# Seven quarter-block products in place of eight for fourteen feed-forward up chunks

## What is computed

```python
D_MODEL, SEQ, D_FF, CONV_WIDTH = 1024, 256, 2816, 3

def _conv_ffn(h, w_up, conv_w, conv_b, w_down):
    up = h @ w_up                       # (256, 1024) @ (1024, 5632)
    C = up.shape[-1]
    rhs = conv_w.reshape(CONV_WIDTH, 1, C).astype(up.dtype)
    up = lax.conv_general_dilated(up, rhs, window_strides=(1,), padding=[(CONV_WIDTH - 1, 0)],
                                  dimension_numbers=('NWC', 'WIO', 'NWC'),
                                  feature_group_count=C) + conv_b
    gate, val = up[..., :D_FF], up[..., D_FF:]
    return (jax.nn.silu(gate) * val) @ w_down
```

## Time and profile before

| | |
|---|---|
| Time, median of 3 runs | 1548.72 us (1547.1 to 1551.06) |
| Time of the profiled execution | 1549.08 us |
| Span of the profiled execution, first to last instruction | 1547.3 us |
| Feed-forward stage on TensorE in the trace | 248.9 to 472.5 us (first up chunk from 241.2) |
| Granted TensorE clock | 0.999 of 2.4 GHz |

### The profile page before, as it was taken

The page is one execution under the profiler, slowest core; times in us unless marked ns, Lnnn a source line. Parts: engine busy times, 40 slices in busy tenths (PEclk is TensorE's granted clock), DMA queues, the critical chain, the costliest instruction groups (busy, mean ns, idle before and its releaser), DMA issues.

```text
span 1547.3 us, 18178 instructions
## 1 busy us (share of the span) xinstructions
PE 1506.0 (97%) x7042; PEld 835.2 (54%) x7042; DVE 468.2 (30%) x894; ACT 320.4 (21%) x660; POOL 22.4 (1%) x43
## 2 busy tenths in 40 slices
PE   9999999999999999899999899999989999999998
PEld 8667888888888755443333243433324433433432
DVE  3665125665642243512121121211211212121112
ACT  2443142111112453211011011101101101110112
POOL 0000000000000000000000000000000000000000
PEclk9999999999999999999999999999999999999999
DMA  9635444777652255899999999999999999999996
GB/s 379 282 111 200 152 167 164 270 274 269 270 194 58 105 216 203 349 399 430 427 428 427 429 419 416 429 427 429 429 428 427 407 427 429 418 429 427 427 429 274
DMA packets 46720, 513.52 MB, mean 332 GB/s; under 512 B 5264, under 2 KB 5408, under 8 KB 8384
## 3 DMA queue, kind: packets, MB, share of 16 engines
q1 hardware_dynamic: 41984, 482.53, 76.1%
q0 software_dynamic: 4672, 30.06, 5.1%
HBM read 511.51 MB, written 1.06 MB: 331 GB/s over the span
## 4 chain that ended last, share of the span: by engine, by line
PE 84%; DMA 11%; DVE 2%; ACT 1%; issue 1%; DVEq 0%; SPq 0%; ACTq 0%
PE bank L1369 33%; PE bank L745 13%; PE bank L1005 9%; DMA ring<-in_up_w 5%; DMA ring<-in_gate_w 5%; PE bank L1014 5%; PE bank L1333 3%; PE bank L1401 3%; PE bank L1491 3%; PE bank L1220 2%; PE bank L856 2%; PE bank L1386 2%; DMA ring<-in_down_w 1%; PE bank L1173 1%; PE bank L1162 1%
## 5 line engine op out<-in xcount | busy, mean ns | idle before, releaser
L1369 PE MATMUL bank<-ring,probs_slab 128*64 128x512 f32 x2824 | 634.9, 597 | 20.4 <-DMA ring<-in_gate_w 11.5
L1369 PEld LDWEIGHTS bank<-ring,probs_slab 128*64 128x64 f32 x2824 | 193.2, 137 | 393.6 <-issue 359.7
L1005 PE MATMUL bank<-normed,ring 128*128 128x256 f32 x672 | 146.9, 379 | 0.0
L2586 DVE TENSOR_TENSOR squares<-bank,tab 128x512 f32<-128x512 f32 x31 | 21.4, 692 | 412.0 <-PE bank L1386 412.0
L1005 PEld LDWEIGHTS bank<-normed,ring 128*128 128x128 f32 x672 | 127.5, 190 | 18.1 <-issue 0.8
L745 PE MATMUL bank<-normed,ring 128*128 128x256 f32 x384 | 84.5, 381 | 0.4 <-ACT normed L1656 0.4
L745 PEld LDWEIGHTS bank<-normed,ring 128*128 128x128 f32 x384 | 72.1, 190 | 11.7 <-ACT normed L1656 1.2
L1014 PE MATMUL bank<-big_slab,ring 128*128 128x256 f32 x352 | 77.6, 379 | 0.0
L1014 PEld LDWEIGHTS bank<-big_slab,ring 128*128 128x128 f32 x352 | 66.9, 190 | 9.1
L2594 DVE TENSOR_TENSOR squares<-bank,tab 128x512 f32<-128x512 f32 x31 | 21.4, 692 | 157.0 <-PE bank L1386 157.0
L2357 DVE SCALAR_TENSOR_TENSOR big_slab<-bank,residual,big_slab 128x255 f32<-128x255 f32 x84 | 40.5, 482 | 83.0 <-ACT big_slab L1818 80.8
(11 more groups left out here) (396 smaller groups left out, 1299.2 us busy)
## 6 DMA issues: line engine op xcount, KB each, us to landing
ring<-in_down_w SPq DMA_DIRECT2D x61, 2048.0 KB, 16.8
ring<-in_up_w SPq DMA_DIRECT2D x60, 2048.0 KB, 18.9
ring<-in_gate_w SPq DMA_DIRECT2D x58, 2048.0 KB, 18.3
ring<-in_front_w SPq DMA_DIRECT2D x72, 1024.0 KB, 5.2
held_slab<-in_mod_w POOLq DMA_DIRECT2D x6, 1024.0 KB, 8.7
memory_slab<-in_mod_w POOLq DMA_DIRECT2D x6, 1024.0 KB, 8.0
cross_keys_slab<-in_mod_w POOLq DMA_DIRECT2D x6, 1024.0 KB, 6.3
probs_turned_slab<-in_mod_w POOLq DMA_DIRECT2D x6, 1024.0 KB, 7.2
```

What stands on the lines that cost most here:

```text
L1005: mm = pe.matmul(bank[bank_at][:, half * T:(half + 1) * T], w[:, (half * DC + k) * P:(half * DC + k + 1) * P], H[:, k, :], start=(k == 0), ...
L1369: mm = pe.matmul(to[half * SLOTS:(half + 1) * SLOTS, :], tokens(k), weights[:, half * D + i * HALF:half * D + (i + 1) * HALF], start=(k == ...
```

## The change

Fourteen up chunks (`SEVEN`: 4 to 11 and 16 to 21) are computed by a scheme of Strassen's kind. The chunk is seen as a 2x2 by 2x2 block product: input features in two halves of 512, output in gate and value, tokens in two halves of 128. In place of eight quarter products there are seven, each four 128x128 blocks of weights against 128 tokens, of sums of quarters of the weights (t1, t2, t4, and one written over the chunk itself in the ring) with sums of quarters of the input (s1 to s4, made once). The results are combined by sums.

VectorE makes the input sums at f = 1, the weight sums of chunk f+2 in the turn of chunk f (four additions of 128x512), and the merge of chunk f (three additions of 128x128 and one of 128x256 that reads PSUM). ScalarE copies parts of the product from PSUM in three steps: `read_first` after the first quarter product, `read_shared` after the fourth, `read_own` at the end. A chunk uses two banks instead of one; two pairs of banks alternate. The combined product lies in `ff_u` in SBUF (one quarter written by `read_own`, three by the merge), and `ff_base` and `ff_taps` read it from there. In ScalarE's order `ff_base(f-1)` now stands behind `read_first(f)`; in VectorE's, `ff_taps(f)` stands behind the gate of f-1 and the weight sums, and the modulation steps behind the taps.

The slabs `HOLD`, `SQ` and `VX` hold the sums, so the modulation has three slabs, its steps are spread anew over the chunks (`MODULATED_AT`), and the three `DFT` transfers are issued when the last up chunk is done, behind all modulation slabs on GpSimd's queue.

```diff
+SEVEN = list(range(4, 12)) + list(range(16, FF_CHUNKS))
+WEIGHT_SUMS, MERGES, _n = {}, {}, 4
+for _f in range(1, FF_CHUNKS):
+    if _f in SEVEN:
+        MERGES[_f] = _n
+        _n += 4
+    if _f + 2 in SEVEN:
+        WEIGHT_SUMS[_f + 2] = _n
+        _n += 4
+MODULATED_AT = {1: [0], 2: [1, 2], 3: [3], 5: [4], 7: [5], 9: [6], 10: [7], 12: [8, 9], 13: [10], 14: [11, 12],
+                15: [13, 14], 16: [15], 17: [16], 18: [17, 18], 19: [19], 20: [20, 21], 21: [22, 23]}
...
-        mod_w = [flat(s, 0, DC) for s in (HOLD, M, KX, PT)]
+        mod_w = [flat(s, 0, DC) for s in (M, KX, PT)]
...
+        ff_b = [[wide(HOLD, 0), wide(HOLD, 2), wide(HOLD, 4)], [wide(HOLD, 6), wide(SQ, 0), wide(SQ, 2)]]
+        ff_a = [wide(VX, 2 * i).rearrange("p (k t) -> p k t", k=4) for i in range(4)]
+        ff_u = [wide(SQ, 4), wide(SQ, 6)]
+        ff_read = [wide(BIG, 14), ff_second_read]
...
-                pool.dma_start(mod_w[n % 4], mod_w_in[n]).then_inc(mod_here[n % 4], 16)
+                pool.dma_start(mod_w[n % 3], mod_w_in[n]).then_inc(mod_here[n % 3], 16)
 
             full(pool, "vx11")
             load_mod(0)
+            pool.wait_ge(s_cross_scored, XHEADS)
             load_mod(1)
-            pool.wait_ge(s_cross_scored, XHEADS)
+            full(pool, "co3")
             load_mod(2)
-            full(pool, "co3")
-            load_mod(3)
+            pool.dma_start(router_w, router_w_in).then_inc(s_in["wr"], 16)
+            pool.dma_start(router_b, router_b_in.partition_broadcast(P)).then_inc(s_in["wr"], 16)
+            for n in range(3, MOD_ROUNDS * DC):
+                pool.wait_ge(s_mod, mod_steps(n - 2))
+                load_mod(n)
+            pool.wait_ge(s_ff_up, FF_CHUNKS)
             pool.dma_start(DFT[:, 0:5, :], dft_in[:, 0:5, :]).then_inc(s_in["dft"], 16)
             pool.dma_start(DFT[:, 6:8, :], dft_in[:, 5:7, :]).then_inc(s_in["dft"], 16)
             pool.dma_start(DFT[:, 5, :], fourier_w_in).then_inc(s_in["dft"], 16)
-            pool.dma_start(router_w, router_w_in).then_inc(s_in["wr"], 16)
-            pool.dma_start(router_b, router_b_in.partition_broadcast(P)).then_inc(s_in["wr"], 16)
-            for n in range(4, MOD_ROUNDS * DC):
-                pool.wait_ge(s_mod, mod_steps(n - 3))
-                load_mod(n)
...
+            def ff_bank_free(f):
+                if f - 2 in SEVEN:
+                    pe.wait_ge(s_ff_sums, MERGES[f - 2] + 4)
+                    pe.wait_ge(s_ff_read, 3 * SEVEN.index(f - 2) + 3)
+                else:
+                    pe.wait_ge(s_ff_conv, f - 1)
+            def ff_seven(f, w):
+                i = SEVEN.index(f)
+                own, shared = bank[2 * (f % 2)], bank[2 * (f % 2) + 1]
+                t1, t2, t4 = ff_b[i % 2]
+                s1, s2, s3, s4 = ff_a
+                def product(to, b, a, start=False):
+                    for k in range(4):
+                        mm = pe.matmul(to, b[:, k * P:(k + 1) * P], a[:, k, :], start=(start and k == 0), stop=True,
+                                       skip_group_check=True)
+                    return mm
+                product(own[:, 0:P], weight_part(w, 0, 0), token_half(0, 0), start=True).then_inc(s_ff_seven, 1)
+                pe.wait_ge(s_ff_sums, WEIGHT_SUMS[f] + 4)
+                product(shared[:, 0:P], t2, s2, start=True)
+                product(shared[:, P:2 * P], weight_part(w, 0, 1), s3)
+                product(shared[:, 2 * P:3 * P], t1, s1).then_inc(s_ff_seven, 1)
+                pe.wait_ge(s_ff_read, 3 * i + 1)
+                product(own[:, 0:P], weight_part(w, 1, 0), token_half(1, 0))
+                pe.wait_ge(s_ff_read, 3 * i + 2)
+                product(shared[:, 2 * P:3 * P], weight_part(w, 1, 1), s4)
+                product(shared[:, P:2 * P], t4, token_half(1, 1)).then_inc(s_ff_up, 1)
...
-                pe.wait_ge(s_ff_conv, 10 + i)
+                pe.wait_ge(s_ff_conv, 11 + i)
...
+            def read_first(f):
+                i = SEVEN.index(f)
+                act.wait_ge(s_ff_seven, 2 * i + 1)
+                if i >= 2:
+                    act.wait_ge(s_ff_sums, MERGES[SEVEN[i - 2]] + 4)
+                act.activation(ff_read[i % 2][:, 0:P], bank[2 * (f % 2)][:, 0:P], ACT.Copy).then_inc(s_ff_read, 1)
+            def read_shared(f):
+                i = SEVEN.index(f)
+                act.wait_ge(s_ff_seven, 2 * i + 2)
+                act.activation(ff_read[i % 2][:, P:4 * P], bank[2 * (f % 2) + 1][:, 0:3 * P],
+                               ACT.Copy).then_inc(s_ff_read, 1)
+            def read_own(f):
+                i = SEVEN.index(f)
+                act.wait_ge(s_ff_up, f + 1)
+                if i >= 2:
+                    act.wait_ge(s_ff_conv, SEVEN[i - 2] + 1)
+                act.activation(ff_u[i % 2][:, 0:P], bank[2 * (f % 2)][:, 0:P], ACT.Copy).then_inc(s_ff_read, 1)
+                act.wait_ge(s_ff_read, 3 * i + 3)
             ff_base(0, 0, 0, True)
-            for f in range(1, 4):
-                ff_base(f, f, f, True)
-                ff_silu(f - 1, f - 1)
-            for f in range(4, FF_CHUNKS):
-                ff_base(f, f % 4, f, False)
+            for f in range(1, FF_CHUNKS):
+                if f in SEVEN:
+                    read_first(f)
+                if f - 1 in SEVEN:
+                    ff_base(f - 1, (f - 1) % 4, f - 1, False)
+                if f in SEVEN:
+                    read_shared(f)
+                else:
+                    ff_base(f, f % 4, f, f < 4)
                 ff_silu(f - 1, (f - 1) % 4)
+                if f in SEVEN:
+                    read_own(f)
                 if f == 11:
                     act.wait_ge(s_mod_sum, 1)
                     act.activation(mod_n[0], bank[1][:, :], ACT.Copy).then_inc(s_mod_read, 1)
+            if FF_CHUNKS - 1 in SEVEN:
+                ff_base(FF_CHUNKS - 1, (FF_CHUNKS - 1) % 4, FF_CHUNKS - 1, False)
...
+            def ff_input_sums():
+                s1, s2, s3, s4 = ff_a
+                dve.tensor_tensor(s1, token_half(0, 1), token_half(1, 1), ADD).then_inc(s_ff_sums, 1)
+                dve.tensor_tensor(s3, token_half(0, 0), token_half(0, 1), SUB).then_inc(s_ff_sums, 1)
+                dve.wait_ge(s_ff_sums, 1)
+                dve.tensor_tensor(s2, s1, token_half(0, 0), SUB).then_inc(s_ff_sums, 1)
+                dve.wait_ge(s_ff_sums, 3)
+                dve.tensor_tensor(s4, token_half(1, 0), s2, SUB).then_inc(s_ff_sums, 1)
+            def ff_weight_sums(f):
+                i = SEVEN.index(f)
+                w, slot, here = ff_ring(f)
+                t1, t2, t4 = ff_b[i % 2]
+                dve.wait_ge(chunk_here[slot], here)
+                if i >= 2:
+                    dve.wait_ge(s_ff_up, SEVEN[i - 2] + 1)
+                b00, b10, b01, b11 = [weight_part(w, k_half, half) for half in range(2) for k_half in range(2)]
+                dve.tensor_tensor(t1, b01, b00, SUB).then_inc(s_ff_sums, 1)
+                dve.wait_ge(s_ff_sums, WEIGHT_SUMS[f] + 1)
+                dve.tensor_tensor(b01, b11, b01, SUB).then_inc(s_ff_sums, 1)
+                dve.tensor_tensor(t2, b11, t1, SUB).then_inc(s_ff_sums, 1)
+                dve.wait_ge(s_ff_sums, WEIGHT_SUMS[f] + 3)
+                dve.tensor_tensor(t4, b10, t2, SUB).then_inc(s_ff_sums, 1)
+            def ff_merge(f):
+                i = SEVEN.index(f)
+                one, six, seventh, fifth = [ff_read[i % 2][:, j * P:(j + 1) * P] for j in range(4)]
+                dve.wait_ge(s_ff_read, 3 * i + 2)
+                dve.tensor_tensor(six, six, one, ADD).then_inc(s_ff_sums, 1)
+                dve.wait_ge(s_ff_sums, MERGES[f] + 1)
+                dve.tensor_tensor(seventh, seventh, six, ADD).then_inc(s_ff_sums, 1)
+                dve.wait_ge(s_ff_sums, MERGES[f] + 2)
+                dve.tensor_tensor(ff_u[i % 2][:, 3 * P:4 * P], fifth, seventh, ADD).then_inc(s_ff_sums, 1)
+                dve.wait_ge(s_ff_up, f + 1)
+                dve.tensor_tensor(ff_u[i % 2][:, P:3 * P].rearrange("p (c n) -> p c n", c=2),
+                                  bank[2 * (f % 2) + 1][:, P:3 * P].rearrange("p (c n) -> p c n", c=2),
+                                  over(six, 2), ADD).then_inc(s_ff_sums, 1)
+                dve.wait_ge(s_ff_sums, MERGES[f] + 4)
+                dve.wait_ge(s_ff_read, 3 * i + 3)
             ff_taps(0, 0)
             dve.wait_ge(s_silu_c, 1)
             for f in range(1, FF_CHUNKS):
-                ff_taps(f, f % 4)
+                if f == 1:
+                    ff_input_sums()
+                if f in SEVEN:
+                    ff_merge(f)
+                else:
+                    ff_taps(f, f % 4)
                 if f > 4:
                     dve.wait_ge(s_ff_down, (f - 1) // 2 - 1)
                 ff_gate(f - 1, (f - 1) % 4)
-                if f <= DC:
-                    modulate(0, f - 1)
-                elif f <= 11:
-                    modulate(1, 2 * (f - 9))
-                    modulate(1, 2 * (f - 9) + 1)
```

(59 more changed lines are left out.)

15 lines of the change are left out of this document (12 added, 3 removed).

## The result

The changed kernel takes 1557.51 us (median of 4 runs, 1555.32 to 1558.84) against 1549.01 before (median of 4 runs); ratio 1.0052, 95% interval 1.004 to 1.0064. It is slower by 8.1 us by the ratio and by 8.5 us by the medians. The profiled execution took 1555.32 us, the shortest of the four, with a span of 1553.4, which is 6.1 more than the span before.

The account below looks back on a forecast made before the run. TensorE's instruction stream was taken to bound the feed-forward stage. Stalls of 13.6 us less 9.0 saved by the products gave net +4.6 on 1549.1, so 1553.7 us, with a range from 1545 to 1561.

Parts of the forecast that it names:

- Bound, and one to one: Feed-forward stage: set by TensorE's instruction stream; the stage's gain or loss passes to the end one to one.
- Products: Up chunks on TensorE: a quarter product takes 0.894 us, seven 6.26 against 6.91, saving 9.0 us over fourteen chunks.
- The stalls: TensorE waits in chunks 5, 7, 9, 11, 17 and before the last down chunk, 12.3 us in sum.
- the restarts: TensorE resuming after each of six stalls: 0.06 us each, 0.4 in all.
- the semaphore waits: Waits held by modulation steps between turns: at 0.04 us each stalls come to 13.3, at 0.1 to 14.6; 13.6 taken.
- the price of a stall: TensorE in the stage: each stall costs its waiting time plus a restart of 0.06 us.
- VectorE some 80% busy: Feed-forward stage: VectorE's busy time goes from 129 us to 186, some 80%.
- At nothing: Input sums, late DFT transfers, router_w and three slabs cost nothing, the slabs while each lands within 9 us.
- Late slabs: Rival, chance 0.12: slabs for steps 14 and 23 take 12 us to land; +11, 1560.
- Dear products: Rival, chance 0.08: products of 128 tokens cost 0.1186 an instruction, 1555, or with weight loads exposed 0.19, 1601.
- an end that isn't tied: Rival, chance 0.06: the experts' stream sets the end whatever the stage does; no change, 1549.
- VectorE keeps up: Rival, chance 0.14 wholly or mostly: VectorE's queue runs 30% quicker than its rows, stalls vanish; 1540.

Follow-up runs that it names:

- the filled gap: Changed kernel with 25 unread 128 by 128 products put on TensorE in the gap before the last down chunk; 1555.89 us, ratio 1.0047.
- the run without a seven-product chunk: Changed kernel with SEVEN empty and modulation steps 22 and 23 moved behind the last gate; 1550.43 us, ratio 1.0006.
- the run of the parts beside the products: Changed kernel with SEVEN empty, keeping three slabs, spread steps, input sums and late tables; 1553.73 us, ratio 1.0031.

## Why the prediction came out as it did

Forecast 1553.7 in 1545 to 1561, slower at 0.51; measured 1557.5, slower. The mechanism held, stalls at the named places that outweigh the saved products; the size was 4 us short, 4.6 forecast against 8.1 by the ratio. The direction was called at little better than even odds, and the part that the forecast had at nothing, the clock, pushed the same way: the call owes something to luck.

**Bound, and one to one.** Right within half a microsecond: a stage shorter by 8.97 made a span shorter by 9.1, and the changed kernel's stage, longer by 6.5, a span longer by 6.1.

**Products.** Right: 0.89 us each. Weight loads of some 192 ns lie under them here too. The 9.03 us are all there once nothing stops them.

**The stalls.** Six gaps at the six places named, each with the releaser named:

| | predicted | start to start |
|---|---|---|
| chunk 5 | 3.0 | 3.2 |
| chunks 7, 9, 11 | 1.0 each | 1.0 each |
| chunk 17 | 0.8 | 1.1 |
| before the last down chunk | 5.5 | 6.1 |
| sum | 12.3 | 13.5 |
| with the restarts (predicted: and the semaphore waits) | 13.6 | 14.0 |

One side remark of the prediction is off: with no step in its turn a chunk would be some 3.5 us early (1.0 late, less a step of 4.54), not 4.5.

**The step that failed** is the price of a stall: the prediction took the waiting time and a restart of 0.06 us, and full clock behind it. The last gap brought the clock down and cost 1.65 us more, as the filled gap shows; a restart in the chunks cost 0.1. With both, the profiled execution comes out: 13.5 - 9.0 + 0.5 + 1.65 = 6.6 against 6.5 at the stage's end. The median is 2.2 above the profiled execution. The other three executions were granted 0.995 of the clock and the profiled one 0.996, so some of it is a lower clock, but that doesn't say where. A fall in chunk 5, seen in two other traces and 1.6 us in one, would be most of it; a fall behind the stage, as in the run without a seven-product chunk, or a slab that comes late at the last gate would do as well. No trace of the changed kernel shows any of the three, so this part stays open.

**VectorE some 80% busy.** Measured 184.29 of 230.00, 80%.

**At nothing.** For the changed kernel this held: no gap was ended by a transfer, on TensorE or on VectorE, and with two steps moved these parts can't be told from the kernel before. For the slabs it held by little: the price of nothing was tied to a landing within 9 us, and in the run of the parts beside the products step 23's slab took 9.6 and held the last gate for 2.9 us.

**Rivals.** Late slabs: excluded for the trace of the changed kernel, where VectorE waits for none; not excluded as a mechanism, since the run of the parts beside the products shows it at work at the last gate. Dear products and an end that isn't tied: excluded. VectorE keeps up: wrong as put, for its instructions have the lengths of the rows; but the 1540 worked out for it came about by another order of the same instructions. I had treated the order as given and not asked what it cost.

What stays open is the scatter, 2 to 7 us among executions of one kernel. Traces show the clock falling near 650 us in two of them and near 1240 us in two; why in one execution and not in the next wasn't tried.

## What to carry to other kernels

Trading products for additions pays only if the adding engine is on time at each hand-over, and its busy share doesn't say so (80% here with 12.5 us of gaps, 86% with none): walk one turn of its queue in order and ask of each piece of work without a near deadline what is queued behind it. Here moving such steps turned +8 us into -9 with the same instructions. Where a forecast leaves a stall on TensorE, price the clock behind it as well as the wait.

## What the runs showed of the hardware

- After 3.0 us without a product the granted clock stayed at 1.00 in the changed kernel's trace and fell to 0.50 at the same place in two others. After a wait of 1.8 us near 650 us it was 1.00 in the trace before and fell to 0.50 in one run (7.09 us of products took 8.78). After 5.9 us it was 0.50, and full again 3.2 us after the products had resumed. A fall cost 1.6 to 2.0 us (a down chunk of 8.56 us behind 5.9 us of gap, one of 8.92 behind 8.8).
- Products of 128x128 weights with 128 tokens kept 0.1117 us an instruction (88 from 276.54 to 286.37 us) with weights from the ring and from slabs that VectorE had just written.
- A 1 MB slab, issued by GpSimd, landed 5.0 to 8.4 us after its issue in the changed kernel's stage, and 5.0 to 10.1 us after it in the kernel before and in the one with the parts but not the products.
